# Moving gate broadcasts and a query transposition from behind an attention to between its batches

## The chip, the cores and the metric

One core of one Trainium2 chip runs the kernel. The metric is device time of one execution in microseconds (us). The engines of the core work from instruction streams of their own and meet only at semaphores: PE is TensorE, DVE is VectorE, ACT is ScalarE, POOL is GpSimd, SP is SyncE, which here only issues transfers.

## The reference

The reference applies two blocks of two layers each to 256 tokens of width 1024, all in fp32. The first block (a sparse attention with a convolution, then a feed-forward and a mixture of experts) is not touched here. The second block has a context of 256 tokens beside the sequence, and per layer a vector of modulations that holds for all tokens, among them two gates `gt1` and `gt2`:

```python
for i in range(DEPTH):                      # DEPTH = 2
    sh1, sc1, gt1, sh2, sc2, gt2 = split(cond @ w_ada[i] + b_ada[i])      # and the same for the context
    a, ac = modulate(h, g_mix[i], sh1, sc1), modulate(hc, g_mix[i], sh1c, sc1c)
    if i == 0: y, yc = swa_mixer(a, ac, ...)   # window attention over sequence and context; context over itself
    else:      y, yc = na_mixer(a, ac, ...)    # neighbourhood attention with a bias; no context output
    h = h + gt1 * y
    h = h + gt2 * swiglu_2(modulate(h, g_ffn[i], sh2, sc2), w_gate_up[i], w_down[i])
    if i == 0:
        hc = hc + gt1c * yc
        hc = hc + gt2c * swiglu_2(modulate(hc, ...), w_gate_up[i], w_down[i])
```

## The kernel before

Tokens lie on the 128 partitions in two halves (`q` = 0 and 1). The second block runs three attentions one after the other: the window attention of layer 0 over the sequence ("sequence attention"), that of the context over itself ("context attention"), and the neighbourhood attention of layer 1. Each has 8 batches of four heads by 128 queries. The keys per query are 512 in the sequence and the neighbourhood attention and 256 in the context's. Every engine's program is written out by hand, so the order of the code is the order of the engine.

In iteration `i` of `attention` PE does `output(i-1)` (L865, L874: probabilities times values, and the row sums spread over the heads), `turn(i)` (L774: the probabilities transposed, in 4 tiles of 128x512, or 2 for the context) and `scores(i+2)` (L824: queries times keys into `pacc`). DVE does `shift(i+1)` (L1787, for the neighbourhood attention also L1803: scores scaled into `prob`, with the row's extreme), then `take_even(i, 0)` (L1843: a turned tile copied to `probT`), `result(i-1)` (L1856), `take_even(i, 2)` where there are four tiles, and `shares(i)` (L1823, L1826). ACT does the exponentials (L1504), copies the odd turned tiles (L1494) and the spread sums (L1514). Turned tiles pass through two PSUM banks, `pt[0]` and `pt[1]`, in turn: PE waits for `bank_emptied`, DVE or ACT for the fill. A batch with 512 keys fills all four banks of `pacc`, so that `scores(i+2)` waits until `shift(i+1)` is done.

In the neighbourhood attention `shift` also waits for a bias, which POOL brings in: 8 transfers (L721) and one addition (L709) per batch, two buffers, started by `bias_used` once the first half of an earlier `shift` is done.

Behind an attention comes `mixer_end`. On PE it first calls `gate_rows` twice (L1340), which spreads the gate vectors over the partitions: each vector of 1024 takes two banks, four matmuls of 128x128 each. DVE copies each bank out in `take_gates` (L2121) to `gateb` and `wv[:, 1, :]` (named `work` in the profile). Then PE waits for `mixed_attn` and projects (`project_out`, L909), and the feed-forward follows (L948 and L962). `gateb` is first used after the first half of the projection, at L2128. In layer 0 the context's queries are also transposed between the sequence attention and `mixer_end`: `turn_heads(bigc, 1536, 0, 16)` on PE (four banks, L774) and `heads_evac` on DVE (L2450), for use in the context attention. The weights of projection and feed-forward come through a ring of six slots that SP fills as slots come free.

Of the kernel before, what the change touches and what calls it, by code (L numbers as in the profile page):

```python
# [26 lines left out]
QT = S // P  # L27
# [167 lines left out]
def scalar_banks():  # L195

    out, n = [], 0

    def vector(count):
        nonlocal n  # L200
        n += count

    def scalar(count=1):
        nonlocal n
        for _ in range(count):
            out.append(n % 2)
            n += 1

    def attend(batches, mods=0):
        for i, b in enumerate(batches):  # L210
            for n in range(b.nkc):
                scalar() if n % 2 else vector(1)
            if i < mods:
                scalar()

    vector(4)
    for l in range(2):
        for item in FRONT[l]:
            scalar() if item == "ada" else vector(2 if item == "kv" else 1)
        vector(1 + 3 + 1)  # L220
        attend(first_batches(), 24 - MODS_EARLY)
    vector(2 + 20)
    for i in range(2):
        for item in QKV[i]:
            if item[0] in "xc":
                scalar() if int(item[1:]) < FIRST_VALUE[i] else vector(1)
            elif item not in ("nc", "nx"):
                vector(2)
        attend(swa_batches(False) if i == 0 else na_batches())
        vector((4, 0)[i] + 2 + 2)  # L230
        if i == 0:
            attend(swa_batches(True))
            vector(2 + 2 + 4)
    return out


def build(nc, a, out):
    ctx = ExitStack()
    with ctx:
# [269 lines left out]
        ffn_at, n = [], 0  # L509
# [217 lines left out]
        def _(pe):  # L727
# [80 lines left out]

            def attention(batches, layer1=False, mods=0, beside=None):
                last = len(batches) - 1  # L810
# [72 lines left out]
                for i in range(last + 1):  # L883
                    if i:
                        output(i - 1)
                    turn(i)
                    if i + 2 <= last:
                        scores(i + 2)
                    if i < mods:
                        ada_tiles(1)  # L890
                output(last)

# [440 lines left out]

            def gate_rows(i, j, s):

                for h in range(2):
                    t, filled, uses, emptied = bank()
# [6 lines left out]

            def turn_heads(src, width, first, nheads, part=None):

                for q in range(QT):
                    for c4 in range(0, nheads // 2, 4) if part is None else (4 * part,):
# [21 lines left out]
            def mixer_end(i, s, src, res, beside=None):  # L1370
                gate_rows(i, 2, s)
                gate_rows(i, 5, s)
                pe.wait_ge(mixed_attn, due("mixed_attn"))
# [3 lines left out]
            for i in range(2):  # L1377
# [15 lines left out]
                for item in QKV[i][:-1]:  # L1393
# [16 lines left out]
                    else:  # L1410
# [5 lines left out]
                        else:  # L1416
                            turn_heads(bigc, 2048, 0, 16, int(item[2]))
                pe.wait_ge(qT_ready, due("qT_ready"))
                attention(swa_batches(False) if i == 0 else na_batches(), layer1=(i == 1),
                          beside=lambda: project(QKV[i][-1]))  # L1420
                if i == 0:
                    pe.wait_ge(heads_ready, 10)
                    turn_heads(bigc, 1536, 0, 16)
                mixer_end(i, 0, hTv, xv)
                if i == 0:
                    pe.wait_ge(qT_ready, due("qT_ready"))
                    pe.wait_ge(sums_taken, QT)
                    attention(swa_batches(True))
                    mixer_end(0, 1, mixed, xcv, beside=turn_ahead)
# [223 lines left out]
        def _(ve):  # L1653
# [112 lines left out]

            def attention(batches, mods=0, beside=None, into=hTv):
                last = len(batches) - 1
# [99 lines left out]
                for i, b in enumerate(batches):  # L1868
# [12 lines left out]
                    elif i < last:  # L1881
                        shares(i + 1)
                result(batches[last])
                ve.sem_inc(mixed_attn, 1)  # L1884
# [229 lines left out]

            def take_gates():

                for gates in (gateb[:, :], wv[:, 1, :]):
                    for h in range(2):
                        t, filled, uses, emptied = bank()
# [322 lines left out]

            def heads_evac(nheads, dst, off=0, part=None):

                for q in range(QT):
                    for c4 in range(0, nheads // 2, 4) if part is None else (4 * part,):
# [9 lines left out]
            def mixer_end(i, s, resv, dst, beside=None):  # L2456
                take_gates()
                if beside is not None:
# [26 lines left out]

            for i in range(2):
                finish = []

# [31 lines left out]
                if i == 0:  # L2520
                    attention(swa_batches(False), beside=lambda: take_heads(i, QKV[i][-1]))
                    heads_evac(16, qTv)
                    tell(qT_ready)
                    end = mixer_end(0, 0, xv, hTv)
                    for q in range(QT):
                        end(q)
                        ve.sem_inc(sums_taken, 1)
                    attention(swa_batches(True), into=mixed)
                    ve.sem_inc(x_ready, QT)
                    ended = mixer_end(0, 1, xcv, mixed, ahead)  # L2530
                else:
                    attention(na_batches(), beside=lambda: take_heads(i, QKV[i][-1]))
                    end = mixer_end(1, 0, xv, hTv)
# [25 lines left out]
```

## Time and profile before

| | |
|---|---|
| median of 3 runs | 3096.09 us (3090.38 to 3101.98) |
| the profiled execution's own time | 3090.59 us |
| its span, first to last instruction | 3088.8 us |
| mean granted TensorE clock | 0.965 of full speed |
| busy: PE, DVE, ACT, POOL | 93%, 24%, 13%, 2% of the span |
| sequence attention, from its first scores until the projection | 1923.90 to 2004.73 us |
| context attention, likewise | 2269.31 to 2313.35 us |
| neighbourhood attention, likewise | 2739.51 to 2821.30 us |

The profile is one execution. Its span runs from the first to the last instruction, and 1.8 us lie around it in the execution's own time. The chain that ended last is followed back from the last instruction, and what stands in it set the end. A value in square brackets at the end of a timeline row is how long the engine was idle before it, and what ended that.

### The profile page before, as it was taken

To read this page: it belongs to the slowest core of one execution; us is meant where nothing else is said; L and a number is where in the kernel's file an instruction comes from. 1 tells how busy PE (TensorE), PEld (TensorE's weight loads), DVE (VectorE), ACT (ScalarE), POOL (GpSimd) and SP (SyncE) were. 2 spreads that over 40 slices of the span, in tenths; PEclk is the share of its full clock that TensorE was granted. 3 is DMA by queue.
4 is the path that set the end of the run, shared out by engine and by line. 5 is a ranking of instruction groups with operands and counts; after the bars stand their busy time and mean duration, and the time that the engine had idled before them with its cause. 6 is when DMAs were issued, how large, how long until landed. Compare 5 with 4: busy or idle time off the path is not lost.

```text
span 3088.8 us, 45002 instructions
## 1 busy us (share of the span) xinstructions
PE 2866.2 (93%) x18895; PEld 1734.1 (56%) x18895; DVE 754.5 (24%) x2060; ACT 409.2 (13%) x972; POOL 68.6 (2%) x96
## 2 busy tenths in 40 slices
PE   4959999995799999999999998899989999988999
PEld 3736777773433333333333357567766777766776
DVE  1762000177331111111111135510042003334001
ACT  1022000102201101101101111400030001023000
POOL 1000000000000000000000010000000000032000
PEclk8979999987899999999999999999999999999999
DMA  9644444573459999999999972044423444132442
GB/s 232 217 131 150 147 152 156 170 217 113 160 186 344 398 381 356 396 378 356 401 376 360 395 243 69 15 136 150 147 71 121 144 157 137 55 83 69 138 148 95
DMA packets 309685, 629.15 MB, mean 204 GB/s; under 512 B 15063, under 2 KB 197599, under 8 KB 293006
## 3 DMA queue, kind: packets, MB, share of 16 engines
q1 hardware_dynamic: 304096, 615.75, 56.1%
q0 software_dynamic: 3136, 8.32, 1.8%
q8 instruction: 134, 2.20, 0.3%
q10 hardware_dynamic: 2286, 2.61, 0.3%
q14 instruction: 33, 0.27, 0.0%
HBM read 621.95 MB, written 4.69 MB: 203 GB/s over the span
## 4 chain that ended last, share of the span: by engine, by line
PE 83%; DVE 9%; issue 2%; DMA 2%; ACT 2%; POOL 1%; SPq 0%; PEld 0%; PEldq 0%; DVEq 0%; POOLq 0%; ACTq 0%
PE pt L948 21%; PE pacc L962 10%; PE pacc L1012 10%; PE pt L801 9%; PE pt L1012 6%; PE pacc L1038 5%; PE pt L1038 5%; PE pacc L909 4%; PE po L1012 3%; PE pt L1250 2%; DVE prob L1787 2%; DVE bigc L2210 2%; DMA ring<-in_w_in 2%; ACT prob L1504 1%; PE pt L757 1%
## 5 line engine op out<-in xcount | busy, mean ns | idle before, releaser
L948 PE MATMUL pt<-hT,ring 128*128 128x256 f32 (+1 forms) x2496 | 505.6, 363 | 5.7 <-DVEq L1675 4.6
L948 PEld LDWEIGHTS pt<-hT,ring 128*128 128x128 f32 x2496 | 444.6, 190 | 77.3 <-issue 19.3
L962 PE MATMUL pacc<-ring,chunks 128*128 128x512 f32 x752 | 330.4, 592 | 0.0
L1898 DVE TENSOR_TENSOR chunks<-chunks,pt 128x256 f32<-128x256 f32 x94 | 39.6, 421 | 884.9 <-ACT chunks L1550 884.9
L962 PEld LDWEIGHTS pacc<-ring,chunks 128*128 128x128 f32 x752 | 142.6, 190 | 159.6 <-issue 146.1
L801 PE MATMUL pt<-ring,hT 128*128 128x256 f32 (+1 forms) x896 | 202.3, 385 | 5.6 <-issue 2.9
L1012 PE MATMUL pacc<-ring,bigc 128*32 128x512 f32 (+1 forms) x1920 | 191.9, 554 | 4.3 <-issue 3.1
L801 PEld LDWEIGHTS pt<-ring,hT 128*128 128x128 f32 x896 | 170.1, 198 | 34.8 <-issue 11.7
L948 PE MATMUL pt<-big,ring 128*128 128x256 f32 (+1 forms) x768 | 156.2, 365 | 2.3 <-DVEq L1675 1.9
L1550 ACT ACTIVATE chunks<-pt 128x256 f32<-128x256 f32 x94 | 36.1, 384 | 908.7 <-PE pt L948 908.7
L948 PEld LDWEIGHTS pt<-big,ring 128*128 128x128 f32 x768 | 137.7, 193 | 24.1 <-issue 6.0
L1012 PE MATMUL pt<-ring,bigc 128*32 128x512 f32 (+1 forms) x1280 | 138.3, 550 | 0.0
L1038 PE MATMUL pacc<-ring,bigc 128*32 128x512 f32 x864 | 137.9, 595 | 0.0
L1012 PEld LDWEIGHTS pacc<-ring,bigc 128*32 128x32 f32 x1920 | 63.2, 110 | 129.7 <-issue 129.7
L1987 DVE TENSOR_TENSOR gateb<-kT,pt 128x512 f32<-128x512 f32 (+1 forms) x32 | 19.9, 621 | 452.4 <-PE pt L1012 451.7
L1038 PE MATMUL pt<-ring,bigc 128*32 128x512 f32 x1056 | 126.6, 593 | 0.0
L1504 ACT ACTIVATE prob<-prob,den 128x256 f32<-128x256 f32 (+3 forms) x192 | 99.2, 518 | 120.2 <-DVEq L1815 115.8
L909 PE MATMUL pacc<-ring,hT 128*128 128x512 f32 x256 | 111.3, 593 | 0.9 <-DVEq L1884 0.9
L801 PE MATMUL pt<-ring,prob 128*128 128x256 f32 x448 | 104.0, 392 | 5.5 <-DVEq L1932 4.0
L774 PE MATMUL pt<-const,prob 128*128 128x128 f32 (+1 forms) x448 | 68.6, 296 | 39.3 <-DVEq L1675 34.2
L2210 DVE SCALAR_TENSOR_TENSOR bigc<-big,convw,bigc 128x256 f32<-128x256 f32 x240 | 100.4, 480 | 3.7 <-DVE hid L2245 0.8
L721 POOL DMA_DIRECT2D biasb<-skew_scratch x64 | 39.0, 618 | 2697.6 <-PE pacc L1038 1774.1
(316 smaller groups left out, 2734.2 us busy)
## 6 DMA issues: line engine op xcount, KB each, us to landing
ring<-in_moe_w_down SPq DMA_DIRECT2D x80, 1024.0 KB, 14.0
ring<-in_w_gate_up SPq DMA_DIRECT2D x66, 1024.0 KB, 5.1
ring<-in_w_ada SPq DMA_DIRECT2D x48, 1024.0 KB, 6.9
ring<-in_moe_w_gate SPq DMA_DIRECT2D x48, 1024.0 KB, 6.5
ring<-in_moe_w_up SPq DMA_DIRECT2D x48, 1024.0 KB, 15.3
ring<-in_w_down SPq DMA_DIRECT2D x33, 1024.0 KB, 4.9
ring<-in_moe_w_gate SPq DMA_DIRECT2D x32, 768.0 KB, 10.2
ring<-in_moe_w_up SPq DMA_DIRECT2D x32, 768.0 KB, 6.5
```

Of the source, the lines that this page charges most:

```text
L774: return pe.transpose(dst, src, ident[0:n, 0:n])
L801: ins = pe.matmul(t[:, q * 256:q * 256 + n], src[:, k, q * P:q * P + P], w[:, k, 0:n], start=(k == 0), stop=(k == KC - 1))
L909: ins = pe.matmul(pacc[:, o:o + 512], src[:, kc, q * P:q * P + P], w[:, k, h * 512:h * 512 + 512], start=(kc == 0), stop=(kc == KC - 1))
L948: ins = pe.matmul(pt[cc][:, j * S + lo:j * S + hi], tiles[j][:, k, cc * P:cc * P + P], src[:, k, lo:hi], start=(k == 0), stop=(k == KC - 1))
L962: ins = pe.matmul(pacc[:, o:o + 512], actb[:, cc * S + q * P:cc * S + q * P + P], tiles[2][:, cc, h * 512:h * 512 + 512], start=(first and ...
L1012: ins = pe.matmul(((X, Y, Z) if kind == "g" else up_bank)[r][32 * j:32 * j + 32, 0:w], hcurv[:, kc, 32 * g:32 * g + 32], moe_view(tile_)[: ...
L1038: ins = pe.matmul(banks[0 if j < 3 else i][32 * j:32 * j + 32, :], actT[:, f, 32 * g:32 * g + 32], w[:, f - 4 * t, :], start=(t == 0 and ( ...
L1250: ins = pe.matmul(t[:, h * S + lo:h * S + hi], w[:, k, h * P:h * P + P], hTv[:, k, lo:hi], start=(k == 0), stop=(k == KC - 1))
L1504: act.activation(prob[:, o:o + b.nk], prob[:, o:o + b.nk], ACT.Exp, scale=-1.0, bias=den[:, 8 + (i % 2) * 4 + j:9 + (i % 2) * 4 + j], accu ...
L1787: return ve.tensor_tensor_reduce(into, out_of, other, -(HD ** -0.5), start, ALU.add, ALU.min, at)
L1898: ve.tensor_tensor(actb[:, cc * S:cc * S + S], sl, pt[cc][:, S:2 * S], ALU.mult)\
L2210: go(ve.scalar_tensor_tensor(out=y[:, cc, :], in0=src, scalar=wk, in1=y[:, cc, :], op0=ALU.mult, op1=ALU.add))
```

## The change

The gates' rows are spread one bank at a time. `gate_rows` and `take_gates` take a step number `n` from 0 to 3, which stands for one half of one gate, and are called at the end of the loop's iterations 0 to 3 of each of the three attentions. The transposition of the context's queries is cut into its two token halves, called at the end of iterations 6 and 7 of the sequence attention. Nothing is computed that was not computed before, and no transfer is touched.

```diff
@@ PE, attention
                         scores(i + 2)
                     if i < mods:
                         ada_tiles(1)
+                    if step is not None:
+                        step(i)
                 output(last)
@@ PE, gate_rows and turn_heads
-            def gate_rows(i, j, s):
-
-                for h in range(2):
+            def gate_rows(i, n, s):
+
+                j = (2, 5)[n // 2]
+                for h in (n % 2,):
                     t, filled, uses, emptied = bank()
@@
-            def turn_heads(src, width, first, nheads, part=None):
-
-                for q in range(QT):
+            def turn_heads(src, width, first, nheads, part=None, tokens=range(QT)):
+
+                for q in tokens:
@@ PE, mixer_end
-                gate_rows(i, 2, s)
-                gate_rows(i, 5, s)
                 pe.wait_ge(mixed_attn, due("mixed_attn"))
@@ PE, layers
+                def gates_and_turns(n):
+                    if n < 4:
+                        gate_rows(i, n, 0)
+                    if i == 0 and n >= 6:
+                        if n == 6:
+                            pe.wait_ge(heads_ready, 10)
+                        turn_heads(bigc, 1536, 0, 16, tokens=(n - 6,))
+
+                def context_gates(n):
+                    if n < 4:
+                        gate_rows(0, n, 1)
+
                 attention(swa_batches(False) if i == 0 else na_batches(), layer1=(i == 1),
-                          beside=lambda: project(QKV[i][-1]))
-                if i == 0:
-                    pe.wait_ge(heads_ready, 10)
-                    turn_heads(bigc, 1536, 0, 16)
+                          beside=lambda: project(QKV[i][-1]), step=gates_and_turns)
                 mixer_end(i, 0, hTv, xv)
                 if i == 0:
                     pe.wait_ge(qT_ready, due("qT_ready"))
                     pe.wait_ge(sums_taken, QT)
-                    attention(swa_batches(True))
+                    attention(swa_batches(True), step=context_gates)
@@ DVE, attention
                     elif i < last:
                         shares(i + 1)
+                    if step is not None:
+                        step(i)
                 result(batches[last])
@@ DVE, take_gates
-            def take_gates():
-
-                for gates in (gateb[:, :], wv[:, 1, :]):
-                    for h in range(2):
+            def take_gates(n):
+
+                for gates in ((gateb[:, :], wv[:, 1, :])[n // 2],):
+                    for h in (n % 2,):
                         t, filled, uses, emptied = bank()
@@ DVE, mixer_end
-                take_gates()
@@ DVE, layers
+                queries = [i == 0]
+
+                def gates_and_turns(n):
+                    if n < 4:
+                        take_gates(n)
+                    if queries[0] and n >= 6:
+                        heads_evac(16, qTv, tokens=(n - 6,))
+                        queries[0] = n == 6
+
-                    attention(swa_batches(False), beside=lambda: take_heads(i, QKV[i][-1]))
-                    heads_evac(16, qTv)
+                    attention(swa_batches(False), beside=lambda: take_heads(i, QKV[i][-1]), step=gates_and_turns)
```

The other attentions get the same `step` on DVE, and `scalar_banks`, which counts the turns of the two banks ahead for ACT, is changed to match.

On PE, in iteration 0 of the sequence attention, before the change (`const,prob` are transposed probabilities, `kT,qT` scores, `probT` the product with the values, `const,den` the spread sums):

```order
L774 MATMUL pt<-const,prob 128x128 x16
L824 MATMUL pacc<-kT,qT 128x512 x4
L865 MATMUL po<-probT,big 64x128 x4
L865 MATMUL po<-probT,bigc 64x128 x4
L865 MATMUL po<-probT,big 64x128 x4
```

The same place after it:

```order
L777 MATMUL pt<-const,prob 128x128 x16
L827 MATMUL pacc<-kT,qT 128x512 x4
L1346 MATMUL pt<-const,mod 128x128 x4
L868 MATMUL po<-probT,big 64x128 x4
L868 MATMUL po<-probT,bigc 64x128 x4
```

Four matmuls of the gates' vector now stand between the scores of batch 2 and the output of batch 0. (An instruction of `order` is one matmul of the program; the profile shows two for each.)

On PE, from the last turned tiles of the sequence attention to the projection, before the change:

```order
L774 MATMUL pt<-const,prob 128x128 x16
L865 MATMUL po<-probT,big 64x128 x4
L865 MATMUL po<-probT,bigc 64x128 x4
L865 MATMUL po<-probT,big 64x128 x4
L865 MATMUL po<-probT,bigc 64x128 x4
L874 MATMUL po<-const,den 64x128 x4
L774 MATMUL pt<-const,bigc 128x128 x16
L1340 MATMUL pt<-const,mod 128x128 x16
L909 MATMUL pacc<-ring,hT 128x512 x24
```

The same place after it:

```order
L777 MATMUL pt<-const,prob 128x128 x16
L777 MATMUL pt<-const,bigc 128x128 x8
L868 MATMUL po<-probT,big 64x128 x4
L868 MATMUL po<-probT,bigc 64x128 x4
L868 MATMUL po<-probT,big 64x128 x4
L868 MATMUL po<-probT,bigc 64x128 x4
L877 MATMUL po<-const,den 64x128 x4
L914 MATMUL pacc<-ring,hT 128x512 x24
```

Half of the query transposes (`bigc`) now stand ahead of the last output, and the projection follows it directly.

On DVE, in iteration 1 of the context attention, before the change (`ISA prob,den` is a `shift` of one head):

```order
L1843 COPY probT<-pt 128x512
L1856 TENSOR_TENSOR big<-po,chunks 128x2x128
L1823 TENSOR_TENSOR den<-den 128x4
L1826 RECIPROCAL den<-den 128x4
L1787 ISA prob,den<-pacc,const,nsink 128x256
```

The same place after it:

```order
L1856 COPY probT<-pt 128x512
L1869 TENSOR_TENSOR big<-po,chunks 128x2x128
L1836 TENSOR_TENSOR den<-den 128x4
L1839 RECIPROCAL den<-den 128x4
L2136 COPY gateb<-pt 128x512
L1800 ISA prob,den<-pacc,const,nsink 128x256
```

The copy of a gate's half now stands ahead of the next `shift`.

## Rows read from the trace of the kernel before

**Rows 1.** The page: span, and shares of the chain that ended last.
```profile
span 3088.8 us, 45002 instructions
PE 83%; DVE 9%; issue 2%; DMA 2%; ACT 2%; POOL 1%; SPq 0%; PEld 0%; PEldq 0%; DVEq 0%; POOLq 0%; ACTq 0%
```

**Rows 2.** The chain, sequence attention, one batch: start us, length us, what.
```profile
1958.82 1.94 PE pacc L824 x8
...
1960.79 0.75 DVE prob L1787
...
1964.02 0.70 DVE probT L1843
...
1964.82 1.09 PE pt L774 x8
...
1967.88 0.75 DVE prob L1787
```

**Rows 3.** The chain, end of the sequence attention.
```profile
1997.54 0.64 PE pt L774 x4
...
2000.68 4.05 PE pt L1340 x32
2004.73 20.60 PE pacc L909 x48
```

**Rows 4.** Timeline, first two gate copies behind the sequence attention.
```profile
2001.87 0.69 DVE L2121 COPY gateb<-pt 128x512 f32<-128x512 f32 x1 [0.47 <-PE pt L1340]
2002.77 0.69 DVE L2121 COPY gateb<-pt 128x512 f32<-128x512 f32 x1 [0.20 <-PE pt L1340]
```

**Rows 5.** Timeline, sequence attention, around PE's last two outputs.
```profile
1987.14 0.69 DVE L1843 COPY probT<-pt 128x512 f32<-128x512 f32 x1
...
1988.24 0.66 PE L865 MATMUL po<-probT,big 128*64 128x128 f32 x8 [1.06 <-ACTq L1531]
...
1994.02 0.66 PE L865 MATMUL po<-probT,big 128*64 128x128 f32 x8 [0.85 <-DVEq L1876]
```

**Rows 6.** The chain, context attention: one batch on DVE, and the end.
```profile
2282.01 0.48 DVE prob L1787
...
2284.17 0.70 DVE probT L1843
...
2286.32 0.48 DVE prob L1787
...
2309.33 4.02 PE pt L1340 x32
```

**Rows 7.** Timeline, context attention, first `shift` inside the loop.
```profile
2277.46 0.48 DVE L1787 CUSTOM_DVE_ANT_0 prob<-pacc,const,nsink 128x256 f32<-128x256 f32 x1 [1.31 <-PE pacc L824]
```

**Rows 8.** Timeline, neighbourhood attention: three `shift`s, and POOL's last two masks.
```profile
2784.79 0.42 DVE L1787 CUSTOM_DVE_ANT_0 prob<-pacc,biasb 128x256 f32<-128x256 f32 x1 [1.26 <-PE pacc L824]
...
2789.07 2.00 POOL L709 TENSOR_TENSOR biasb<-biasb,const 128x1024 f32<-128x1024 f32 x1 [1.77 <-DMA biasb<-skew_scratch]
...
2792.25 0.42 DVE L1787 CUSTOM_DVE_ANT_0 prob<-pacc,biasb 128x256 f32<-128x256 f32 x1 [1.26 <-PE pacc L824]
...
2797.66 2.00 POOL L709 TENSOR_TENSOR biasb<-biasb,const 128x1024 f32<-128x1024 f32 x1 [1.78 <-DMA biasb<-skew_scratch]
...
2799.81 0.42 DVE L1787 CUSTOM_DVE_ANT_0 prob<-pacc,biasb 128x256 f32<-128x256 f32 x1 [1.35 <-PE pacc L824]
```

**Rows 9.** The chain, end of the neighbourhood attention.
```profile
2817.28 4.02 PE pt L1340 x32
```

**Rows 10.** Windows: stretch, us, busy us (count) by engine, granted clock, DMA share, GB/s.
```profile
1940.00:1946.50 6.50, 4.67 (x15) 1.91 (x14) 1.03 (x3) 2.41 (x7) 0.00 (x0) 0.52 0.01 1
...
1954.00:1990.00 36.00, 31.33 (x342) 23.50 (x338) 25.11 (x70) 24.14 (x63) 0.00 (x0) 1.00 0.00 1
```

**Rows 11.** Timeline: PE behind two pauses, and scores at the lower clock.
```profile
1939.17 0.91 PE L774 MATMUL pt<-const,prob 128*128 128x128 f32 x4 [3.05 <-DVEq L1675]
...
1942.95 3.60 PE L824 MATMUL pacc<-kT,qT 64*128 64x512 f32 x8
...
2302.97 1.09 PE L865 MATMUL po<-probT,bigc 128*64 128x128 f32 x16 [1.76 <-DVEq L1876]
```

More of the change, by code:

```diff
@@ L207, in scalar, with attend @@
             n += 1
-    def attend(batches, mods=0):
+    def attend(batches, mods=0, rows=0, turns=False):
         for i, b in enumerate(batches):
@@ L214, in attend @@
                 scalar()
+            if i < rows:
+                vector(1)
+            if turns and i >= 6:
+                vector(2)
     vector(4)
@@ L228, in scalar_banks @@
                 vector(2)
-        attend(swa_batches(False) if i == 0 else na_batches())
-        vector((4, 0)[i] + 2 + 2)
+        attend(swa_batches(False) if i == 0 else na_batches(), rows=4, turns=(i == 0))
         if i == 0:
-            attend(swa_batches(True))
-            vector(2 + 2 + 4)
+            attend(swa_batches(True), rows=4)
+            vector(4)
     return out
@@ L807, in mark_used, with attention @@
                 pe.drain().then_inc(tile_used, 1)
-            def attention(batches, layer1=False, mods=0, beside=None):
+            def attention(batches, layer1=False, mods=0, beside=None, step=None):
                 last = len(batches) - 1
@@ L1765, in rotate, with attention @@
                 settle()
-            def attention(batches, mods=0, beside=None, into=hTv):
+            def attention(batches, mods=0, beside=None, into=hTv, step=None):
                 last = len(batches) - 1
@@ L2441, in take_heads, with heads_evac @@
                 return finish
-            def heads_evac(nheads, dst, off=0, part=None):
-                for q in range(QT):
+            def heads_evac(nheads, dst, off=0, part=None, tokens=range(QT)):
+                for q in tokens:
                     for c4 in range(0, nheads // 2, 4) if part is None else (4 * part,):
@@ L2527, in _ @@
                         ve.sem_inc(sums_taken, 1)
-                    attention(swa_batches(True), into=mixed)
+                    attention(swa_batches(True), into=mixed, step=gates_and_turns)
                     ve.sem_inc(x_ready, QT)
@@ L2531, in _ @@
                 else:
-                    attention(na_batches(), beside=lambda: take_heads(i, QKV[i][-1]))
+                    attention(na_batches(), beside=lambda: take_heads(i, QKV[i][-1]), step=gates_and_turns)
                     end = mixer_end(1, 0, xv, hTv)
```

## The prediction

> **What bounds the kernel now.** I read the page first, then the chain of waits over the three attentions of the second block, then the timeline inside them, and last the windows for the clock. On the whole span the chain that ended last is PE for 83% and DVE for 9% [rows 1]. That average says little here: in the feed-forwards PE never pauses, but in the attentions the chain goes back and forth between PE and DVE. One batch of the sequence attention reads: PE scores 1.94 us, DVE `shift` from 1960.79, DVE copy of the first turned tile at 1964.02, PE transposes that needed its bank at 1964.82, PE scores again, next `shift` at 1967.88 [rows 2]. So a batch costs 7.09 us, and it is a closed loop with no slack: whatever stands between the end of the scores and the next `shift` lengthens it. The neighbourhood attention has the same loop with 7.46 us (2784.79 to 2792.25), DVE idle for 1.26 us before each `shift` because PE is still at the scores [rows 8]. The context attention is different: there DVE hardly rests, 4.31 us from `shift` to `shift` [rows 6].
>
> **What is removed.** Behind the sequence attention PE starts on the query transposes at 1997.54, on the gate matmuls at 2000.68 and on the projection at 2004.73 [rows 3]. All of this lay on the chain, and the projection only needs `mixed_attn`, which DVE gives right behind `output_taken`, for which PE already waited before 1997.54. So 7.19 us go there. Behind the context attention it is 4.02 us [rows 6], behind the neighbourhood attention 4.02 us [rows 9]. Together 15.2 us, which is 0.49% of the kernel: the whole gain that the edit can have. What follows is not freed further. The projection and the feed-forward are the same PE work, and their weights come in by the same transfers; DMA engines were 0.00 to 0.01 busy through the sequence attention [rows 10], so the ring was full and waiting.
>
> **What is added in the sequence attention, iterations 0 to 3.** The code puts the gate matmuls behind `scores(i+2)` on PE, and the copy behind `shares(i)` on DVE, where DVE's next instruction is `shift(i+2)`. That `shift` needs just those scores. DVE works in program order, so it now waits past the end of the scores for the gate matmuls, copies, and only then shifts. The rows behind the attention give the sizes: from the start of the gate matmuls at 2000.68 [rows 3] to the copy of the first bank at 2001.87 is 1.19 us, and from copy to copy, with its semaphores, 0.90 us [rows 4]. That makes 2.09 us. The first gate matmul can follow while the last score matmul drains, for which I take off 0.1, so 2.0 us per step. The banks are no further wait: a gate's bank is the one of the third turned tile, which DVE has emptied during the scores. PE has gained work too, but after the gate it needs 0.9 us (its share of 4.05) plus output and the first transposes before DVE wants a tile, and DVE is itself 2.0 late by then; PE is not the later one. The queue behind the waiting copy is `shift`, then ACT's exponentials, both one batch late together. Bounds: 0.9 us if the matmuls were hidden and only the copy counted, 2.9 us if the matmuls ran at the lower clock. Four steps: +8.0 us.
>
> **Iterations 6 and 7.** The turns stand between `turn` and `output`. PE can start on them when DVE has emptied the bank, after the copy at 1987.14 of 0.69 us, and two banks of transposes take 1.09 us as they do in [rows 2]. That ends at about 1989.0, where `output(6)` began at 1988.24 [rows 5]: 0.75 us late. Before `output(7)`, at 1994.02, PE waits as well, and half of the 1.09 us should fit in: 0.45 us. DVE's four copies lie in its waits for PE. Together +1.2 us, between 0 and 2.2. Sum for the sequence attention: 8.0 + 1.2 - 7.19 = +2.0 us.
>
> **Context attention.** In iteration 0 DVE waits for the scores, 1.31 us until 2277.46 [rows 7], so that step costs 2.0 us as above. Later DVE is the later engine. PE has the scores done before DVE has finished `result` and `shares`, so the gate's bank is mostly full when DVE comes, and the copy costs its 0.90 us. The bank must first be emptied by the tile copy at 2284.17; from there to the next `shift` at 2286.32 are 2.15 us [rows 6], of which the copy takes 0.8 and the gate's fill 1.19, so it just fits. 2.0 + 3 x 0.9 = 4.7; less 4.02 it is +0.7 us (bounds: 3.6 if all four steps cost the copy alone, 8.0 if all wait).
>
> **Neighbourhood attention.** The same 2.0 us for each step, 8.0 us. Only the last `shift` waited for POOL, whose mask ran from 2797.66 to 2799.66 while the loop alone would have asked at 2792.25 + 7.46 = 2799.71; it started at 2799.81 [rows 8]. So 0.1 us is absorbed. POOL's next batch is released by `shift`s that come up to 8 us later, but one of its batches takes 8.59 us (2789.07 to 2797.66 [rows 8]): released some 1.5 us into the `shift` of 2784.79, now 8 us later, it ends its last mask at about 2803, before 2807.7, when the late loop asks. 8.0 - 0.1 - 4.02 = +3.9 us.
>
> **Sum.** 2.0 + 0.7 + 3.9 = +6.6 us. On the profiled execution, 3090.59 us, that is 3097.2. This execution was at the fast end of the runs: the median of the three is 3096.09, 5.5 us above it. Against the median the sum is 3102.7, and since the profiled execution counts as a fourth run near the low end, I say 3102.
>
> **Rival 1, the gates hide.** The pauses of PE and DVE in the loop swallow the steps, and the 15.2 us are all gained: 3096 - 15 = 3081. For it: DVE is idle 1.26 us before each `shift` of the neighbourhood attention [rows 8], more than a copy. Against it: that idle time ends with the scores, and the gate matmuls come after the scores, so the copy can't use it. If half of it held, 3088 or so. 8 in 100.
>
> **Rival 2, POOL is the bound of the neighbourhood attention.** Its 8.59 us per batch are longer than the loop's 7.46 [rows 8], so late `shift`s might cost nothing and only the 4.02 us remain: 3102.7 - 7.9 = 3094.8. Against it: POOL entered with two batches in hand and met the loop only at its last mask, by 0.1 us. 5 in 100.
>
> **Rival 3, the clock falls: slower.** TensorE stood at 0.52 of its clock from 1940 to 1946.5, that is 1.2 GHz instead of 2.4, behind a pause of 3.05 us, and at 1.00 from 1954 to 1990 [rows 10, 11]. In the longer batches PE pauses more: some 0.7 us of the 7.09 before, about 1.8 after. One batch of the context attention had a pause of 1.76 us and ran on at the full rate, 16 matmuls in 1.09 us [rows 11]. At the lower clock the scores take 3.60 us [rows 11] where 1.94 stood [rows 2], the transposes 1.1 and the gate 1.0 more: about 3.7 us per batch. Three such batches add 11 us and bring the total to +18, over 0.5%; all eight of the sequence and neighbourhood attentions that have gates give 3132. 9 in 100. The Trainium skill, page "TensorE: Matmul & The Clock Gate", section "Why this matters for your kernels", advises against long PE pauses between bursts of matmuls, because the clock falls back to its lower level. [...]
>
> **Chances and range.** My forecast, +3 to +10 us with its terms at their likely ends, has 78 in 100. A measurement of this kernel, whose runs lie 0.37% apart, tells about 0.5% (15.5 us) from no change. The forecast lies inside, and most of rivals 1 and 2 as well, since the whole gain is 0.49%: faster 0.04, same 0.88, slower 0.08, the last from rival 3. The forecast's own range, with 4 us for the scatter of medians, is 3094 to 3109. To leave out no more than 2 in 10 I take 3090 to 3112: down to half of rival 1, up to two batches at the low clock.
>
> **What would show it.** In the profile after, the `shift`s of iterations 2 to 5 of the sequence attention should lie 9.1 us apart instead of 7.09, each behind a copy to `gateb` or `work`, and DVE should wait for the gate matmuls before each copy. In the neighbourhood attention 9.5 instead of 7.46. In the context attention 5.2 instead of 4.31. The projection should begin 1.1 us after the last output in all three. First scores to projection: 80.8 us becomes 82.8, 44.0 becomes 44.7, 81.8 becomes 85.7. I am wrong if a gate copy costs the loop less than 1.5 us where PE bounds it, if the granted clock is under 0.9 in these loops outside their first batch, or if something else in the span moves: the feed-forwards, the first block and the experts should be the same to a microsecond.

## The result, and the profile after

The changed kernel's median is 3109.9 us (3103.45 to 3113.04, 6 runs) against 3093.24 us (3087.02 to 3102.34, 6 runs) of the kernel before: ratio 1.0038, 95% interval 1.0023 to 1.0054, that is 7 to 17 us slower. The two medians alone lie 16.7 us apart, at the upper end of that interval. Run once more among the experiments it gave 1.0027 (1.0012 to 1.0042). It is slower, by the ratio less than the 0.5% that I counted as no change, and its median is inside the stated range of 3090 to 3112. I had forecast +6.6 us and a total of 3102.

The page of the changed kernel: its span, the clock granted to TensorE in 40 slices, and the shares of its chain:

```profile
span 3108.9 us, 45002 instructions
...
PEclk8969999986899999999999999999999999999999
...
PE 84%; DVE 9%; issue 2%; DMA 2%; ACT 2%; PEld 0%; SPq 0%; PEldq 0%; DVEq 0%; ACTq 0%
```

POOL's 1% of [rows 1] is gone from the chain. The span is 20.1 us longer than in [rows 1], more than the medians say. Of these, 10.4 us had come up before the sequence attention's first scores (at 1934.29 us instead of 1923.90), in a part that nobody touched. So I read the three attentions by themselves. The table has the time from the first score matmul on PE's timeline to the first matmul of the projection:

| profile | first scores at | sequence | context | neighbourhood | ratio to before (95%) |
|---|---|---|---|---|---|
| before | 1923.90 | 80.7 | 43.9 | 81.7 | |
| before, again | 1930.84 | 80.5 | 43.9 | 81.4 | 1.0001 (0.9988 to 1.0014) |
| changed | 1934.29 | 82.9 | 45.0 | 87.8 | 1.0038 (1.0023 to 1.0054) |
| changed, again | 1936.36 | 82.7 | 46.6 | 87.8 | 1.0027 (1.0012 to 1.0042) |
| e2, turns only | 1932.51 | 78.7 | 43.9 | 81.9 | 1.0006 (0.9990 to 1.0021) |
| e7, gates only | 1931.22 | 84.1 | 46.5 | 87.9 | 1.0036 (1.0022 to 1.0050) |
| e3, copy after shift | 1931.51 | 78.6 | 45.2 | 81.9 | 0.9999 (0.9986 to 1.0012) |
| e4, third bank | 1926.67 | 74.5 | 46.4 | 76.5 | 0.9979 (0.9965 to 0.9993) |
| e5, pauses | 1935.66 | 74.9 | 42.2 | 78.3 | 0.9962 (0.9946 to 0.9977) |
| e8, filler | 1932.47 | 82.9 | 46.4 | 84.7 | 1.0027 (1.0012 to 1.0041) |
| e9, copy twice | 1932.28 | 88.8 | 45.8 | 87.8 | 1.0041 (1.0025 to 1.0057) |

In the changed kernel the sum over the three is +9.5 us in the first profile and +10.8 in the second. That lies inside the intervals of the two ratios, which are worth 11.8 and 8.4 us.

The chain in the sequence attention of the changed kernel, from one `shift` to the next (start, length, what; `prob L1800` is the `shift`):

```profile
1964.26 1.92 PE pacc L827 x8
1966.17 1.10 PE pt L1346 x8
...
1967.30 0.70 DVE gateb L2136
...
1968.17 0.75 DVE prob L1800
...
1972.21 1.09 PE pt L777 x8
1973.30 1.92 PE pacc L827 x8
1975.22 1.10 PE pt L1346 x8
...
1977.22 0.75 DVE prob L1800
```

Set beside [rows 2] these show the cost of a step: between the scores and the `shift` there are now the gate matmuls (1.10 us) and the copy with its semaphores (0.87 us). The pitch, from `shift` to `shift`, is 9.05 us instead of 7.09, so a step costs 1.96; I had said 2.0.

The end of that attention:

```profile
2013.48 1.90 PE po L868 x32
2015.38 0.46 PE po L877 x8
...
2017.19 7.96 PE pacc L914 x18
```

Nothing stands between the last output and the projection but the wait for the result. It takes 1.35 us, where PE waited 1.11 us before the transposes in the kernel before (1996.42 to 1997.54). Behind the context attention the wait has grown more:

```profile
2328.68 10.54 PE L914 MATMUL pacc<-ring,big 128*128 128x512 f32 x24 [1.74 <-DVEq L1899]
```

In the neighbourhood attention it is not so simple. A pause of PE in its loop before the change, then PE's timeline in the changed kernel:

```profile
2789.19 1.09 PE L774 MATMUL pt<-const,prob 128*128 128x128 f32 x8 [1.09 <-DVEq L1675]
```

```profile
2777.44 0.66 PE L868 MATMUL po<-probT,big 128*64 128x128 f32 x8
...
2779.78 1.09 PE L777 MATMUL pt<-const,prob 128*128 128x128 f32 x8
2782.90 1.86 PE L777 MATMUL pt<-const,prob 128*128 128x128 f32 x8 [2.03 <-DVEq L1688]
2784.70 2.85 PE L827 MATMUL pacc<-kT,qT 64*128 64x512 f32 x8
2787.47 1.16 PE L1346 MATMUL pt<-const,mod 128*128 128x128 f32 x8
...
2794.02 1.09 PE L777 MATMUL pt<-const,prob 128*128 128x128 f32 x8 [2.03 <-DVEq L1688]
2795.05 1.99 PE L827 MATMUL pacc<-kT,qT 64*128 64x512 f32 x8
...
2803.51 1.97 PE L777 MATMUL pt<-const,prob 128*128 128x128 f32 x8 [2.03 <-DVEq L1688]
2805.41 2.73 PE L827 MATMUL pacc<-kT,qT 64*128 64x512 f32 x8
```

And the windows over the same three batches (after the five engines' busy times: granted clock, DMA share, GB/s):

```profile
2778.50:2789.60 11.10, 9.07 (x77) 6.46 (x75) 5.85 (x21) 4.62 (x11) 6.88 (x9) 0.85 0.23 48
2789.60:2799.10 9.50, 7.47 (x78) 5.54 (x76) 5.85 (x21) 4.62 (x11) 4.91 (x8) 1.00 0.27 57
2799.10:2810.20 11.10, 9.07 (x78) 6.58 (x75) 5.85 (x21) 4.62 (x11) 8.84 (x10) 0.85 0.23 48
```

Every batch has a pause of 2.03 us in it, where 1.09 us stood before. Behind the first and the third, the same 8 transposes take 1.86 and 1.97 us instead of 1.09, and the scores 2.85 and 2.73 instead of 1.99. The clock of 0.85 over 11.1 us amounts to some 3.3 us at 1.2 GHz, and the batch reads 11.1 us instead of 9.5. The second pause of the same length left the clock at 1.00.

### The profile page after: what moved, and what is told of

Its sections match the earlier page's. It is cut to its first block, busy times and chain, and to the rows that moved or that the text cites. A ratio compares the mean times of both kernels' runs of the same rounds, so it can differ in the third digit from the quotient of the medians.

```text
span 3108.9 us, 45002 instructions
## 1 busy us (share of the span) xinstructions
PE 2877.6 (93%) x18895; PEld 1741.6 (56%) x18895; DVE 754.5 (24%) x2060; ACT 409.4 (13%) x972; POOL 69.2 (2%) x96
## 4 chain that ended last, share of the span: by engine, by line
PE 84%; DVE 9%; issue 2%; DMA 2%; ACT 2%; PEld 0%; SPq 0%; PEldq 0%; DVEq 0%; ACTq 0%
PE pt L953 21%; PE pacc L967 10%; PE pacc L1017 9%; PE pt L804 9%; PE pt L1017 6%; PE pacc L1043 5%; PE pt L1043 5%; PE pacc L914 4%; PE po L1017 3%; DVE prob L1800 2%; PE pt L1255 2%; DMA ring<-in_w_in 2%; DVE bigc L2225 2%; PE pacc L827 1%; PE pt L777 1%
## 5 line engine op out<-in xcount | busy, mean ns | idle before, releaser
L804 PEld LDWEIGHTS pt<-ring,hT 128*128 128x128 f32 x896 | 169.9, 198 | 34.8 <-issue 11.8
```

What stands on the lines that cost most here:

```text
L804: ins = pe.matmul(t[:, q * 256:q * 256 + n], src[:, k, q * P:q * P + P], w[:, k, 0:n], start=(k == 0), stop=(k == KC - 1))
```

## The experiments

**e1, before again.** The kernel before, unchanged.

> The kernel before, once more, to see what its parts scatter by. The profile of the changed kernel has its last projection of queries ahead of the sequence attention 10.4 us later than before, in a part that was not touched. Theory A (scatter: dips of TensorE's clock and the pace of the transfers in the first block): this run starts its sequence attention anywhere from 0 to 10 us off the first profile of before (first scores at 1923.9 us), and its three attentions, from first scores to projection, read 80.8, 44.0 and 81.8 us again, to 2 us. Theory B (the change slows the first block, by code that lies elsewhere): this run's first scores stay within 2 us of 1923.9. Ratio 1.000 either way.

Its attentions read 80.5, 43.9 and 81.4 us, and its first scores came at 1930.84 us, 6.9 us later than in the first profile of the same kernel. So theory B is out: this part of the program scatters by itself. In all eleven profiles of the table the first block is the same code, and the sequence attention starts anywhere between 1923.9 and 1936.4 us. Two profiles of one kernel differ by 6.9 us here; the other 3.5 of the 10.4 us can't be told apart from chance with so few profiles. An edit of this size is better read from the parts than from the span of one profile.

**e2, turns only.** The gate rows stand behind the attentions as before; the two token halves of the query transposition stay in iterations 6 and 7.

```diff
                 def gates_and_turns(n):
-                    if n < 4:
-                        gate_rows(i, n, 0)
                     if i == 0 and n >= 6:
...
             def mixer_end(i, s, src, res, beside=None):
+                for n in range(4):
+                    gate_rows(i, n, s)
```

> Only the query transposes are moved to iterations 6 and 7; the gate rows stay behind the attentions as before. By my terms the turns cost 1.2 us inside (PE late by 0.75 and 0.45 us) and save 3.14 us behind (1997.54 to 2000.68), so the sequence attention reads 78.9 us from first scores to projection instead of 80.8; the other two as before, 44.0 and 81.8. Ratio 0.999 to 1.000. Rival (any matmul put into the loop costs what it takes, wherever it stands): the turns cost their 2.2 us of PE and about 3.6 us of DVE copies inside, and the sequence attention reads 79.9 to 81.3 us.

Measured 78.7, 43.9 and 81.9 us. The sequence attention is 2.0 us shorter than in the first profile before and 1.8 us shorter than in e1; 1.2 us of cost against 3.14 saved makes 1.9. The rival, 79.9 us or more, is out. The profile shows this net gain; it is too small for the ratio (1.0006) to show.

**e7, gates only.** The reverse: the turns behind the attention, the gates in it.

```diff
-                    if i == 0 and n >= 6:
-                        if n == 6:
-                            pe.wait_ge(heads_ready, 10)
-                        turn_heads(bigc, 1536, 0, 16, tokens=(n - 6,))
...
+                if i == 0:
+                    pe.wait_ge(heads_ready, 10)
+                    turn_heads(bigc, 1536, 0, 16)
                 mixer_end(i, 0, hTv, xv)
```

> Only the gate rows are moved; the query transposes stay behind the sequence attention. Sequence attention 82.9 + 3.14 - 1.3 = 84.8 us from first scores to projection (steps 8.0 us inside, 4.05 us saved behind), context 45.0, neighbourhood 85.4 to 87.8. Ratio to the kernel before 1.003 to 1.005. If instead the gates in the loop were cheap and the turns dear, the sequence attention would read 81 us or less.

Measured 84.1, 46.5 and 87.9 us, ratio 1.0036: 12.3 us more than before over the three. All of the loss is in the gates.

**e3, copy after shift.** PE's program is that of the changed kernel; on DVE the copy of a gate's half moves behind the next `shift`.

```diff
                     if i and i < last:
                         shift(i + 1)
+                    if step is not None and 1 <= i <= 4:
+                        step(i - 1)
                     take_even(b, 0)
...
-                    if step is not None:
+                    if step is not None and i >= 4:
                         step(i)
```

> The changed kernel with one edit: DVE copies a gate's half behind the next shift instead of ahead of it (and ahead of the next tile copy). PE's program is the same. Theory 1 (a step costs 2.0 us because the shift stands behind a wait for the gate matmuls, 1.1 us, and behind the copy, 0.9 us): the wait goes and the copy stays, so the pitch of the shifts in iterations 2 to 5 falls from 9.05 to 8.0 us in the sequence attention and from 9.5 to 8.4 in the neighbourhood attention; first scores to projection 78.6, 44.0 and 81.5 us, 9 us less than the changed kernel in all. Theory 2 (the added PE work or the longer pauses of the loop cost the time, wherever DVE's copy stands): pitch stays at 9 us and nothing is gained. Ratio to the kernel before 0.999 by theory 1, 1.004 by theory 2.

DVE's timeline in the sequence attention of this kernel:

```profile
1954.09 0.75 DVE L1800 CUSTOM_DVE_ANT_1 prob<-pacc,const,nsink 128x512 f32<-128x512 f32 x1 [4.48 <-PE pacc L827]
...
1957.31 0.69 DVE L2138 COPY gateb<-pt 128x512 f32<-128x512 f32 x1
1958.15 0.69 DVE L1856 COPY probT<-pt 128x512 f32<-128x512 f32 x1
...
1962.13 0.75 DVE L1800 CUSTOM_DVE_ANT_1 prob<-pacc,const,nsink 128x512 f32<-128x512 f32 x1 [1.18 <-PE pacc L827]
...
1970.17 0.75 DVE L1800 CUSTOM_DVE_ANT_0 prob<-pacc,const,nsink 128x512 f32<-128x512 f32 x1 [1.17 <-PE pacc L827]
```

The pitch is 8.04 us, 1.01 less than in the changed kernel with the same instructions. DVE again waits for the scores and no longer for the gate. In the neighbourhood attention the pitch is 8.41 with no batch of 11: PE's matmuls are the same, but its pauses in the loop are 0.44 and 0.18 us, and its clock is 1.00 from 2775 to 2808 us. Measured 78.6 (expected 78.6) and 81.9 (expected 81.5). The context reads 45.2 where I had expected 44.0: there the copy costs 0.84 us (pitch 5.15 instead of 4.31) in this place as in the other. The ratio, 0.9999, says that the change made with this order is no change.

**e4, third bank.** The gates get a PSUM bank of their own (`pada`, unused in this block) and a pair of semaphores; in the attentions with four tiles their matmuls stand between the second and the third tile of `turn`.

```diff
-                    t, filled, uses, emptied = bank()
-                    pe.wait_ge(emptied, uses)
+                    t = pada[:, :]
+                    if gates_spread[0]:
+                        pe.wait_ge(gate_emptied, gates_spread[0])
+                    gates_spread[0] += 1
...
                         ins.then_inc(odd_filled if t_ % 2 else filled, 1)
+                        if t_ == 1 and b.nkc == 4 and between is not None:
+                            between(i)
```

> The changed kernel with the gate rows in a PSUM bank of their own, which the second block leaves unused, and in the two attentions with four tiles the gate matmuls stand between the second and the third tile of turn, where PE waits 0.7 us for DVE in the kernel before. DVE copies at the end of the iteration as in the changed kernel, but the bank is then long full. Theory 1: matmuls 0.9 us against 0.7 us of pause cost 0.2 to 0.3 us per step, the copy of 0.9 us fits into the 1.06 us that DVE waits for the scores, so the pitch is 7.3 us (sequence) and 7.6 us (neighbourhood); first scores to projection 76.0 and 79 us, context 44.7 as in the changed kernel. In all 7 to 9 us less than the kernel before: ratio 0.997. Theory 2 (what is added costs the loop its own time, 0.9 us of PE and 0.9 us of DVE): pitch 8.9 us or more, ratio 1.002 to 1.004.

PE in the sequence attention of this kernel, from its timeline:

```profile
1958.24 1.09 PE L777 MATMUL pt<-const,prob 128*128 128x128 f32 x8
1959.16 1.06 PE L1355 MATMUL pada<-const,mod 128*128 128x128 f32 x8
1960.06 1.09 PE L777 MATMUL pt<-const,prob 128*128 128x128 f32 x8
1961.08 1.99 PE L827 MATMUL pacc<-kT,qT 64*128 64x512 f32 x8
1962.99 0.66 PE L870 MATMUL po<-probT,big 128*64 128x128 f32 x8
```

and DVE:

```profile
1956.02 0.75 DVE L1809 CUSTOM_DVE_ANT_1 prob<-pacc,const,nsink 128x512 f32<-128x512 f32 x1 [0.22 <-PE pacc L827]
...
1962.20 0.69 DVE L2147 COPY work<-pada 128x512 f32<-128x512 f32 x1
1963.11 0.75 DVE L1809 CUSTOM_DVE_ANT_0 prob<-pacc,const,nsink 128x512 f32<-128x512 f32 x1 [0.22 <-PE pacc L827]
```

The pitch is 7.09 us, that of the kernel before: the gate step costs nothing. The matmuls have taken PE's pause (no idle time stands in its rows), and the copy has taken DVE's wait for the scores, of which 0.22 us is left. I had allowed 0.2 to 0.3 us per step. Measured 74.5 and 76.5 us, better than the 76.0 and 79 expected. The context's four steps still stand where they did; it reads 46.4 us, between the 45.0 and 46.6 of the changed kernel, where I had expected 44.7. e4 changes the place of the matmuls and their bank together; which of the two is needed was not tested.

**e5, pauses.** As e4, and the context's steps moved: PE spreads the first half before the first scores, the second in iteration 1, the third in iteration 7, the fourth behind the last output; DVE copies in iterations 0, 6 and 7 and beside the projection.

```diff
+                    gate_rows(0, 0, 1)
                     pe.wait_ge(qT_ready, due("qT_ready"))
...
                 def context_gates(n):
-                    if n < 4:
-                        gate_rows(0, n, 1)
+                    if n in (1, 7, 8):
+                        gate_rows(0, {1: 1, 7: 2, 8: 3}[n], 1)
...
+            def context_gates(n):
+                if n in (0, 6, 7):
+                    take_gates({0: 0, 6: 1, 7: 2}[n])
```

> As e4_third_bank, and in the context attention the four steps lie in pauses: the first half's matmuls ahead of the first scores, where PE waits 2.8 us for DVE, its copy in iteration 0; the second half's matmuls in iteration 1 and its copy in iteration 6; the third half in iteration 7; the matmuls of the fourth behind the last output, where PE waits 1.1 us for the result, and its copy beside the projection. Theory 1 (only work that stands between the scores and the next shift, or on DVE in this attention, costs time): first scores to projection 40 to 41 us instead of 43.9, the others as in e4_third_bank, 74.5 and 76.5 us. Sum against the kernel before: 15 us less, ratio 0.995. Theory 2 (the pauses were needed, and the work turns up elsewhere): 43 us or more, ratio 0.998 as e4_third_bank.

The context reads 42.2 us instead of 46.4 in e4 and 43.9 before: a gain, but 1 to 2 us short of what I expected. PE behind the last pauses of this kernel's context attention:

```profile
2309.40 1.86 PE L870 MATMUL po<-probT,bigc 128*64 128x128 f32 x16 [1.77 <-DVEq L1902]
...
2311.04 1.07 PE L879 MATMUL po<-const,den 128*64 128x128 f32 x8
2312.04 1.53 PE L777 MATMUL pt<-const,prob 128*128 128x128 f32 x8
```

The same 16 matmuls took 1.09 us at the same place in the kernel before [rows 11], behind a pause of 1.76 us; here the clock was down, and it still was for the spread sums (1.07 instead of 0.61 us) and the transposes (1.53 instead of 1.09). The three rows are 1.7 us longer, about what is missing. The neighbourhood attention reads 78.3 us where I had expected the 76.5 of e4, with the same code in it. There the clock was at 0.86 from 2812 to 2822 us, and from the last `shift` to the projection it took 17.72 us instead of 16.07. Over the three attentions e5 has 10.8 us less than the kernel before, not the 15 that I expected. Its ratio to the kernel before is 0.9962, so it beats both kernels: the one before by 0.4% and the changed one, by the quotients with its two ratios, by 0.6 to 0.8%.

**Changed kernel again.** To see whether the 11 us batches come back.

> The changed kernel once more, for its parts. Its first profile read 82.9, 45.0 and 87.8 us from first scores to projection; the last is 2.1 us over my 85.7, with TensorE at 0.88, 0.92 and 0.81 of its clock in three of the windows of its lengthened batches. If the dips are chance, this profile's neighbourhood attention reads 85.4 us plus 1.8 us for each dip it happens to have, and the sequence attention 82.9; if the longer pauses bring them on every time, it reads 87.8 again. Ratio 1.002 to 1.005.

It read 87.8 us again, with `shift`s at the same distances: 11.13, 9.49 and 11.10 us here, 11.12, 9.49 and 11.11 in the first profile, 11.13, 9.49 and 11.12 in e7. e9 below leaves this attention as it is in the changed kernel and has 11.12, 9.49 and 11.12. Four profiles agree, so in this loop the dips are not chance.

**e8, filler.** The changed kernel with extra matmuls: in iterations 1 to 4 of the neighbourhood attention PE multiplies a constant by itself four times, behind the second tile, into a bank that nobody reads. Their result is used nowhere.

```diff
                         ins.then_inc(odd_filled if t_ % 2 else filled, 1)
+                        if b.bias and t_ == 1 and 1 <= i <= 4:
+                            for k in range(4):
+                                pe.matmul(pada[:, k * P:k * P + P], ident, ident, start=True, stop=True)
```

> The changed kernel with 16 matmuls more than it needs: in iterations 1 to 4 of the neighbourhood attention PE runs four extra 128x128 matmuls of a constant, into a PSUM bank that nobody reads, behind the second tile of turn, where it pauses 2.03 us for DVE. In three profiles of the gates in this loop the pitch of the shifts was 11.1, 9.5 and 11.1 us, each time to 0.02 us, and TensorE's clock stood at 0.53 to 0.57 of full speed behind the first and the third of these pauses. Theory P (the lengthened pause of PE lets the clock fall, rival 3 of the prediction in small): with the pause cut to 1.1 us the clock stays at 1.00 and all three pitches are 9.5 us; first scores to projection 84.6 us instead of 87.8, although PE does more. Theory D (the bias transfers, 0.5 of the DMA engines busy in those windows, or something else that comes every second batch slows PE down): 87.8 us again. Ratio to the kernel before 1.002 by P, 1.0035 by D.

PE's timeline, and the window over the three batches:

```profile
2790.52 1.09 PE L777 MATMUL pt<-const,prob 128*128 128x128 f32 x8
2791.45 1.06 PE L850 MATMUL pada<-const 128*128 128x128 f32 x8
2793.65 1.09 PE L777 MATMUL pt<-const,prob 128*128 128x128 f32 x8 [1.14 <-DVEq L1691]
2794.67 1.99 PE L827 MATMUL pacc<-kT,qT 64*128 64x512 f32 x8
```

```profile
2783.00:2809.00 26.00, 22.58 (x219) 17.29 (x220) 15.26 (x54) 12.87 (x31) 18.51 (x25) 1.00 0.29 61
```

The clock is 1.00 throughout, the `shift`s are 9.49 us apart three times, and the attention reads 84.7 us (expected 84.6) instead of 87.8. PE does more and the loop is 3.1 us shorter. The transfers ran as before (0.29 of the DMA engines), so theory D is out. The filler shortens PE's pause and gives it more work at once; which of the two keeps the clock up is not told apart. The ratio, 1.0027, is the lower of the two that the changed kernel had and can't show 3 us.

**e9, copy twice.** The changed kernel; each gate copy of the sequence attention is done twice, so that PE's pause grows. The second copy writes the same values.

```diff
+                        if twice:
+                            link(ve.tensor_copy(gates[:, 512 * h:512 * h + 512], t[:, :]))
                         go(ve.tensor_copy(gates[:, 512 * h:512 * h + 512], t[:, :]))
```

> The changed kernel, with each of the four gate copies of the sequence attention done twice on DVE. No transfers run there. The pause of PE per batch grows from 1.59 us (clock 1.00 throughout in the changed kernel) to about 2.4 us, longer than the 2.03 us of the neighbourhood attention. Theory P: the clock now falls here as well, in at least one of the three batches behind the first, and the pitches read 9.9 us in some and 11.5 us in others. Theory D (transfers): 9.9 us in all three, four extra copies at 0.8 us, 3.2 us in all and no more.

PE's timeline, sequence attention:

```profile
1961.86 1.97 PE L777 MATMUL pt<-const,prob 128*128 128x128 f32 x8 [2.31 <-DVEq L1688]
1963.76 2.69 PE L827 MATMUL pacc<-kT,qT 64*128 64x512 f32 x8
...
1973.20 1.09 PE L777 MATMUL pt<-const,prob 128*128 128x128 f32 x8 [2.31 <-DVEq L1688]
1974.22 1.99 PE L827 MATMUL pacc<-kT,qT 64*128 64x512 f32 x8
...
1992.74 1.97 PE L777 MATMUL pt<-const,prob 128*128 128x128 f32 x8 [2.31 <-DVEq L1688]
1994.64 2.60 PE L827 MATMUL pacc<-kT,qT 64*128 64x512 f32 x8
```

```profile
1962.00:1966.00 4.00, 4.00 (x16) 2.46 (x16) 1.42 (x4) 2.02 (x5) 0.00 (x0) 0.60 0.02 6
1972.00:1990.00 18.00, 14.48 (x142) 10.87 (x143) 11.44 (x27) 8.82 (x23) 0.00 (x0) 1.00 0.00 1
1992.50:1997.00 4.50, 4.26 (x16) 2.59 (x16) 1.59 (x5) 2.33 (x8) 0.00 (x0) 0.62 0.02 4
```

The clock fell here as well, behind the first and the fourth of the lengthened pauses (0.60 and 0.62 in these windows), with 0.02 of the DMA engines busy. The `shift`s lie 11.33, 9.78, 9.77 and 8.59 us apart. The attention reads 88.8 us: 5.9 more than in the changed kernel, of which 3 are the copies. So a longer pause of PE brings the dips about, in another attention and without transfers. But the two pauses between them, equally long, left the clock at 1.00, so the pause alone does not say which batch is hit.

## Why the prediction was right, and where it was off

**The range and the number.** By the ratio the change costs 11.8 us (7 to 17), by the three attentions 9.5 and 10.8, and by the medians 16.7; all are above the 6.6 that I forecast. The median of 3109.9 also lies above 3109, the end of the forecast's own range. It is inside 3112 because I had widened the range to allow for two batches at the low clock. Two such batches did come, at under half of their price, so the range held for a reason that was in it; that the median stayed inside by 2 us is partly luck.

**The bound and what is removed.** Right but for the wait in front of the projection. The loop between PE and DVE had no slack, and the matmuls behind the attentions are gone. But I had said that the projection begins 1.1 us after the last output in all three. It began 1.35 us after it behind the sequence and the neighbourhood attention and 1.71 us behind the context, so 0.24, 0.24 and 0.6 us of the 15.2 came back.

**A step of the gates.** Right in size and in its two parts. 2.0 us were forecast, 1.96 measured in the sequence attention (pitch 9.05 instead of 7.09). e3 takes the wait for the matmuls away (1.01 us) and leaves the copy; e4 hides both, and the cost is 0.00. (The gate's share of 4.05 us is 1.0 us and not the 0.9 that I wrote; no term hangs on it.) So rival 1, the hidden gates, is not wrong as an idea: the pauses are there. But the change puts its steps behind the scores, with which the pauses end.

**Iterations 6 and 7.** Right as far as the net shows: 1.2 us forecast, and e2 reads 78.7 us (78.9 expected). With four steps of 8.0 us, 1.2 for the turns and 0.24 for the wait, less 7.19, the sequence attention comes to the +2.2 us that it has.

**Context attention.** +0.7 us forecast; +1.2 in the first profile, +2.7 in the second. The steps cost 4.4 us together, a little less than the 4.7 forecast: the later ones lengthen the way from `shift` to `shift` from 4.31 to 5.15 us, the copy's 0.84. What I missed is the end, 0.8 us longer than without the gates' 4.02, of which the wait is 0.6. The two profiles differ only there: 10.7 us from the last `shift` to the projection in the first, 12.2 in the second. The clock was at 1.00 from 2318 to 2329 us in the one and at 0.86 from 2320 to 2332 in the other, so here a dip comes in some executions and not in others.

**Neighbourhood attention.** This is the term that was mis-sized: +3.9 us forecast, +6.1 measured, in four profiles (87.8, 87.8, 87.9 and 87.8 us). The steps cost 2.0 us as computed (9.49 instead of 7.46), and POOL's last mask ended 2.7 us before its `shift`. On top come 1.6 us in each of two batches, in which the clock fell; the sum had nothing for that. At the end of this attention the kernel before had a dip of its own (0.86 of its clock from 2805 to 2817), which the changed one lacks: from the last `shift` to the projection it was 21.33 us, 17.31 without the gates' 4.02, and is 16.06 now, which gives 1.25 us back. e4 and e5, whose code is the same there, have 16.07 and 17.72, so this part can be chance. I had the mechanism as rival 3, at 3.7 us per batch and with a chance of 9 in 100. The runs show it as a fixed part of this loop, at under half of that price. I had put the pause of the longer batches at about 1.8 us, from the 0.7 of the sequence attention. It became 1.59 us there, and the clock stayed at 1.00; in the neighbourhood attention, where 1.09 us stood before, it became 2.03. My precedent, the pause of 1.76 us with the clock at 1.00 [rows 11], was a single case, and e5 shows the clock down behind a pause of 1.77 us at the same place. I had written that I would be wrong if the granted clock was under 0.9 outside the first batch; it was 0.85 in two. The Trainium skill, "TensorE: Matmul & The Clock Gate", section "Why this matters for your kernels", advises against idle gaps of TensorE between bursts of matmuls, but only against longer ones than the 2.03 us of this loop. e8 and e9 agree with its direction, by 3.1 us won with the pause filled and some 3 lost with it drawn out; they don't agree with the length that it allows.

**Rival 2.** Out: the page of the changed kernel has no POOL in its chain, and every `shift` of the neighbourhood attention found its mask done.

**The total.** 6.6 + 2.2 (neighbourhood) + 0.5 (context) + 0.2 (sequence) makes the 9.5 us of the first profile. I had said that everything else would be the same to a microsecond, and it was not: besides the 10.4 us of the first block the stretch between the first two attentions was 1.7 us longer and that between the last two 1.6 us shorter, which cancel. e1 shows such steps without any change: its stretch between the last two attentions is 3.3 us shorter than in the first profile of the same kernel (423.0 us instead of 426.3), and its first block 6.9 us longer.

## What to carry to other kernels

When work is moved into a loop that goes back and forth between two engines, find the pause of each engine and put each engine's share of the work into it. Here the pause of PE lay before the third tile and that of DVE before the end of the scores; with the matmuls in the one, the copy in the other and a bank of their own (e4), a step cost nothing. The same work behind the scores stood in front of the `shift` and cost 1.96 us a step. So a copy should not stand ahead of the instruction that the loop waits for if what it copies is made only after the loop's own work. And a loop that is lengthened by one engine can draw out the pauses of TensorE: read the granted clock batch by batch. Here a pause of 2 us cost 1.6 us more in two of three batches, the same two in every profile of that code.

## What was not expected of the hardware

Useless matmuls shortened the neighbourhood attention: 16 extra ones (four in each of four batches, 0.9 us per batch) took 3.1 us off it, with TensorE's clock at 1.00, that is 2.4 GHz, over the three batches of which two had dipped. For the whole program the ratio does not show it. The dips in the loop of the neighbourhood attention repeat in four profiles, batch for batch, to 0.02 us, while those at the ends of the context and the neighbourhood attention come and go with the same code. Within one profile pauses of equal length (2.03 us, 2.31 us) are followed by either clock. What decides between them stays open.
